# A large SBUF region moved from 64 bytes past a multiple of 128 to a multiple of 128, in a two-block transformer kernel

## What is computed

```python
# first block
h = rmsnorm(x) ; q, k, v, g, u, sv, a_ret, a_sgu = split(h @ w_in)
y_ret = (layernorm(retention(rotary(q), rotary(k), v)) * silu(g)) @ w_ret_o
y_sgu = (gelu(u) * (w_spatial mixed over layernorm(gelu(sv)) + b)) @ w_sgu_o
merged = sigmoid(a_ret) * y_ret + sigmoid(a_sgu) * y_sgu
x = x + rmsnorm(merged @ w_out)
a, b = split(conv3(rmsnorm(x) @ w_up) + conv_b)       # 1024 -> 2 * 2816
x = x + rmsnorm((gelu(a) * b) @ w_down)               # 2816 -> 1024
# second block: top-k sparse attention and sliding-window attention, gated
x = x + (sigmoid(g_a) * (o_a @ w_branch_a) + sigmoid(g_b) * (o_b @ w_branch_b)) @ w_out_2
x = x + relu(rmsnorm(x) @ w_up_2) ** 2 @ w_down_2     # 1024 -> 4096 -> 1024
return rmsnorm(x)
```

## Time and profile before

| | |
|---|---|
| time, median of 3 runs | 1735.6 us (1735.3 to 1737.29) |
| span of the profiled execution | 1735.5 us |
| instructions | 19726 |
| TensorE matmuls busy (PE) | 1653.0 us |
| TensorE weight loads busy (PEld) | 1347.8 us |
| VectorE (DVE) | 830.2 us |
| ScalarE (ACT) | 449.3 us |
| GpSimd (POOL) | 908.1 us |
| mean granted TensorE clock | 0.969 of full speed |

### The profile page before, as it was taken

How to read it: one execution, slowest core, us unless ns; L and a number is a source line. 1 busy time by engine, 2 the same in 40 slices (tenths; PEclk the granted TensorE clock), 3 DMA queues, 4 the chain that set the end, 5 groups by cost and what they waited for, 6 DMA issues and landing times.

```text
span 1735.5 us, 19726 instructions
## 1 busy us (share of the span) xinstructions
PE 1653.0 (95%) x7556; PEld 1347.8 (78%) x7556; DVE 830.2 (48%) x1094; ACT 449.3 (26%) x742; POOL 908.1 (52%) x336
## 2 busy tenths in 40 slices
PE   7999999999998999999989898589999899999998
PEld 6887888888887888888878776467677788888886
DVE  6702688510836666660032999944546532013302
ACT  3012112101114344441131222033331243123312
POOL 5873386877784444444474555403137544444442
PEclk9999999999999999999999999779899999999999
DMA  5332032332222333332212212101012222223221
GB/s 196 96 124 70 25 103 73 122 97 97 97 85 86 97 97 97 97 97 97 97 65 88 76 52 95 49 1 49 25 49 97 74 73 97 101 93 98 97 97 73
DMA packets 123281, 147.48 MB, mean 85 GB/s; under 512 B 5142, under 2 KB 98374, under 8 KB 123206
## 3 DMA queue, kind: packets, MB, share of 16 engines
q1 hardware_dynamic: 121622, 141.90, 25.3%
q10 hardware_dynamic: 1584, 4.52, 0.7%
HBM read 144.31 MB, written 2.10 MB: 84 GB/s over the span
## 4 chain that ended last, share of the span: by engine, by line
PE 82%; DVE 12%; POOL 3%; issue 2%; ACT 1%; DMA 0%; SPq 0%; DVEq 0%; POOLq 0%; ACTq 0%
PE ps L522 24%; PE ps L523 24%; PE ps L524 24%; PE ps L811 3%; PE ps L822 2%; DVE work L1516 2%; PE ps L701 2%; DVE top L1513 2%; DVE score L1505 2%; PE ps L816 1%; POOL w_lo L471 1%; PE ps L631 1%; POOL w_hi L462 1%; DVE m_lo L1401 1%; DVE rope_u L1273 1%
## 5 line engine op out<-in xcount | busy, mean ns | idle before, releaser
L471 POOL TENSOR_TENSOR w_lo<-raw,w_hi 128x1024 fp32r<-128x1024 f32 (+2 forms) x260 | 650.4, 2523 | 402.8 <-ACT w_hi L880 397.6
L462 POOL TENSOR_TENSOR w_hi<-raw,cells 128x2048 fp32r<-128x2048 f32 (+1 forms) x67 | 246.3, 3676 | 402.3 <-PE ps L522 402.3
L522 PE MATMUL ps<-hT_hi,w_hi 128*128 128x512 f32 (+1 forms) x960 | 372.3, 388 | 1.0 <-DVE hT_lo L1225 0.5
L523 PE MATMUL ps<-hT_lo,w_hi 128*128 128x512 f32 (+1 forms) x960 | 370.2, 386 | 0.0
L524 PE MATMUL ps<-hT_hi,w_lo 128*128 128x512 f32 (+1 forms) x960 | 369.6, 385 | 0.0
L522 PEld LDWEIGHTS ps<-hT_hi,w_hi 128*128 128x128 f32 x960 | 183.3, 191 | 38.4 <-issue 1.9
L524 PEld LDWEIGHTS ps<-hT_hi,w_lo 128*128 128x128 f32 x960 | 183.0, 191 | 35.6
L523 PEld LDWEIGHTS ps<-hT_lo,w_hi 128*128 128x128 f32 x960 | 183.3, 191 | 35.1
L880 ACT ACTIVATE w_hi<-raw 128x2048 fp32r<-128x2048 f32 x63 | 120.2, 1908 | 209.6 <-PE ps L522 207.9
L523 PE MATMUL ps<-w_lo,f_hi 128*128 128x512 f32 x432 | 170.2, 394 | 0.0
L522 PE MATMUL ps<-w_hi,f_hi 128*128 128x512 f32 x432 | 169.3, 392 | 0.0
(11 more groups left out here) (256 smaller groups left out, 2196.4 us busy)
## 6 DMA issues: line engine op xcount, KB each, us to landing
raw<-in_w_in SPq DMA_DIRECT2D x86, 512.0 KB, 4.5
raw<-in_w_up SPq DMA_DIRECT2D x76, 512.0 KB, 4.5
raw<-in_w_down SPq DMA_DIRECT2D x54, 512.0 KB, 4.0
raw<-in_w_out SPq DMA_DIRECT2D x16, 512.0 KB, 3.8
raw<-in_w_ret_o SPq DMA_DIRECT2D x8, 512.0 KB, 4.4
raw<-in_w_sgu_o SPq DMA_DIRECT2D x8, 512.0 KB, 4.4
x<-in_x SPq DMA_DIRECT2D x4, 512.0 KB, 7.4
raw<-in_w_branch_b SPq DMA_DIRECT2D x4, 512.0 KB, 4.4
```

Source lines behind the costliest of these rows:

```text
L462: nc.gpsimd.tensor_tensor(w_hi[:, s, 0:n], raw[:, s, 0:n], zero.broadcast_to([P, n]), ALU.add).then_inc(unit_hi, 1)
L471: nc.gpsimd.tensor_tensor(w_lo[:, s, c], raw[:, s, c], w_hi[:, s, c].bitcast(f32), ALU.subtract).then_inc(unit_split, 1)
L522: first = nc.tensor.matmul(dst, a_hi, b_hi, start=start, stop=False)
L523: nc.tensor.matmul(dst, a_hi, b_lo, start=False, stop=False)
```

## The change

`cells` gets 176 words instead of 192, so that the region behind it begins 64 bytes lower. The one cell in use beyond 176, `zero`, moves to an unused one.

```diff
         conv = at("conv", [P, 4, 2 * FB], small0 + 3072)
-        cells = at("cells", [P, 192], small0 + 3776)
-        A = small0 + 3776 + 768
+        cells = at("cells", [P, 176], small0 + 3776)
+        A = small0 + 3776 + 704
         eps = cells[:, 0:1]
...
-        zero = cells[:, 176:177]
+        zero = cells[:, 2:3]
```

## The result

| | before | after |
|---|---|---|
| median of 20 runs | 1736.62 us (1735.3 to 1737.98) | 1739.51 us (1737.72 to 1743.08) |
| span of the profiled execution | 1735.5 us | 1738.0 us |
| after / before, 95% interval | | 1.0016 [1.0011, 1.0022] |

The forecast was 1729.1 us, with a range of 1727.0 to 1736.0, and 0.05 for slower by over 0.2%. The result lies outside the range and on the other side: 1739.51 - 1736.62 = 2.9 us lost, with an interval of 0.11% to 0.22%. It is slower clear of noise, though by less than the 0.2% from which the prediction counts a version as slower. Instructions and their order on each engine are those of before.

What follows compares the result with a forecast made beforehand. TensorE was taken to bound the kernel, with the chain on it for 82% of the span. Gains of 1.26 + 1.26 + 0.96 + 1.06 + 0.34 + 0.85 + 0.79 = 6.5 us took 1735.6 to 1729.1 us, range 1727 to 1736.

Steps and rivals of the forecast that it cites:

- the distance between the operands is what counts: Rival: the penalty grows with the operands' distance inside 256 bytes and doubles, another 6.5 us lost, 1742.1 us; chance 0.05.
- the low bits don't matter: Rival: the address's low bits have no effect and nothing changes, 1735.6 us; chance 0.15. `iq_ik`'s pace was counted for it.
- terms 1 and 2: `y_ret` and `y_sgu`, streaming from `A`: each falls from 44.80 to 43.54 us, a gain of 1.26 us each.
- term 3: `out1`, holding `mT`: 146 matmuls before the chain leaves TensorE, by 6.6 ns, a gain of 0.96 us.
- Terms 4 to 6: Stages holding tiles from `A`: gains of 1.06 us in `down1`, 0.34 in `out2`, 0.85 and 0.79 in the two `down2`.
- `zero` at nothing: GpSimd's `w_hi`, which reads the moved cell `zero`: no cost taken, at most 4.8 us lost.
- VectorE and ScalarE at nothing: `oT_lo` on VectorE and `out_rows` on ScalarE, both in `A`: already as fast as in the fixed part, so no gain.
- Plain fp32 matmuls at nothing: TensorE's transposes, mix and attention values: no gain taken from alignment, though up to 0.9 us was possible.
- The doubt about `mT` and `f`: A penalty of the low bits alone should be equal for both held tiles, but is 6.7 and 2.2 ns.
- or at 240 (the distance does): Sign in `y_ret`: a pace of 240 ns means the distance counts, 233.3 ns that the low bits don't matter.

Runs made afterwards that it cites:

- Experiment 3: TensorE alone, none of the kernel's work: eight moving by eight stationary starts, 32 bytes apart within 256; 226.7 ns with both at 64, 232.7 with moving 128 and stationary 0.
- Experiment 9: TensorE alone, none of the kernel's work: fp32r matmuls with other column counts at several distances, and `iq_ik` at its own addresses; 328 columns spread over 6.6 ns, `iq_ik` took 151.0.
- experiment 1: TensorE alone, none of the kernel's work: stretches of 48 matmuls at the kernel's addresses before and after; holding `f` took 228.7 ns before, 233.3 after.
- change again: The changed kernel run and profiled once more, against the kernel before; 1739.73 us, ratio 1.0018 [1.0008, 1.0028].
- `A` at 448: Kernel before with `cells` packed into 112 words and `A` 256 bytes below the change's, again distance 128; 1739.77 us, ratio 1.0016 [1.0007, 1.0026].
- `zero` alone: Kernel before with only the cell `zero` moved, to cell 2; 1736.59 us against 1736.57, ratio 1.0001 [0.9992, 1.001].
- packed alone: Kernel before with `cells` packed into 112 words and `A` left at its place; 1736.77 us, ratio 1.0002 [0.9992, 1.0011].
- `A` at 640: Kernel before with `cells` packed into 112 words and `A` 64 bytes above `w` modulo 256 instead of 64 below; 1740.18 us, ratio 1.0023 [1.0014, 1.0033].
- `A` at 576: Kernel before with `cells` packed into 112 words and `A` 128 past a multiple of 256, like `w`: distance 0; 1729.46 us, ratio 0.9954 [0.994, 0.9967].
- The version with all at multiples of 256: Kernel before with `cells` packed into 112 words, `A` where the change put it and `BASE` raised by 128: distance 0; 1728.79 us, ratio 0.9955 [0.9941, 0.9968].
- the two controls: Kernel before with only `zero` moved (1736.59 us, ratio 1.0001), and with `cells` packed into 112 words but `A` in place (1736.77 us, ratio 1.0002).
- experiment 7: TensorE alone: chains of 96-matmul stages without pause at the addresses of before; `mT` took 233.4 ns after `yT`, 228.9 after `hT`.
- 6: TensorE alone: finer distances, fewer columns, plain fp32, and stages with all slots and PSUM banks; 512 columns of fp32r took 226.7 ns at distance 0, 232.3 at 4.

## Why the prediction was wrong

**The step that failed** is the one named as the step that it takes: that the move "gives each of the slow stretches the pace that the same shape has with both operands at multiples of 128, 226.7 ns". The earlier trace rows hold only three combinations, and in the fast one both operands lie 128 past a multiple of 256. "Both at a multiple of 128" and "both at the same place within 256 bytes" fit these rows equally well. The edit separates them: it puts `A` at a multiple of 256 and leaves `w` 128 from it. Experiment 3 decides for the second reading.

**The evidence against the right rival.** The prediction names it ("the distance between the operands is what counts"), gives it 0.05, and holds `iq_ik` against it: distances of 32 to 96 bytes at 150.5 ns. That 328 columns without a loss take about that long was the author's estimate; the rows of before hold no other pace at this column count to measure it by. Experiment 9 shows 150.0 at distance 0 for 328 columns, and more at 32 (153.3) but less at 224 (146.7), so the row could neither confirm nor exclude anything at 512. The same row was counted for "the low bits don't matter", as wrongly.

**The rival's price was off too.** It let the penalty grow with the distance, to 240 ns and 1742.1 us. The measured paces are 228.9 at 192 (233.3 for `mT`), 233.3 at 64 and 232.2 to 233.3 at 128. So what streams `oT` or `yT` went from one slow place to another and stayed (233.3), and only what holds `f` or `m` lost, 3.5 ns a matmul.

**The terms of the sum.** With the places right they were good. At distance 0 the gain is 1736.53 - 1729.46 = 7.1 us for 6.5 forecast, with an interval of 5.7 to 10.4, and the five stretches have the lengths that the terms assume. In the change, with minus for a gain: terms 1 and 2 (`y_ret`, `y_sgu`) came out at 0 for -1.26 each, term 3 (`out1`) at 0 for -0.96. Terms 4 to 6 changed sign: `down1` 482 matmuls by 3.5 ns, +1.69 for -1.06; `out2` 155 by 3.2 (from the 229.0 and 232.2 of its addresses in experiment 1), +0.50 for -0.34; the two `down2` 768 by 3.5, +2.69 for -1.64. By paces that makes 4.9 us, and 2.9 were measured.

**Where the other 2 us are.** The start or end of a stage in each profile, less the same in the profile of before, in us:

| | change, change again, `A` at 448 | `zero` alone, packed alone | `A` at 640 | `A` at 576 |
|---|---|---|---|---|
| end of `down1` | +1.59, +1.43, +1.58 | -0.26, -0.32 | +0.07 | -5.28 |
| first matmul of the second block (919.61 before) | +0.38, +0.19, +0.35 | -0.56, -0.58 | -0.08 | -5.19 |
| start of `y_a` (1293.96 before) | -0.17, -0.52, -0.41 | -0.72, -0.62 | +0.09 | -5.55 |
| start of the first `down2` | -0.13, -0.40, -0.33 | -0.52, -0.43 | +0.36 | -5.45 |
| end of the last `down2` | +2.56, +2.30, +2.37 | -0.52, -0.43 | +3.79 | -7.16 |

The loss of both `down2` (2 x 1.34 = 2.7) arrives in full. That of `down1` is there at its end and gone by the first `down2`, in all three profiles at distance 128. With `A` at 640 and at 576 what `down1` lost or gained is kept.

The boundary behind `down1` shows where 1.1 us of it come back. The rows run from the transposes (L631) of the last rows of `x` to the transposes that follow, in before, packed alone, the change and `A` at 640:

```profile
912.44:918.82 6.38, 6.38 (x21) 5.33 (x22) 2.68 (x4) 1.19 (x2) 0.00 (x0) 0.55 0.34 106
912.11:918.24 6.13, 6.13 (x21) 5.13 (x22) 2.69 (x4) 1.19 (x2) 0.00 (x0) 0.57 0.35 110
913.88:919.20 5.32, 5.32 (x21) 4.48 (x21) 2.69 (x4) 1.19 (x2) 0.00 (x0) 0.68 0.40 128
912.31:918.74 6.43, 6.43 (x21) 5.40 (x22) 2.69 (x4) 1.19 (x2) 0.00 (x0) 0.54 0.33 104
```

TensorE does the same work in each and has no gap. What differs is the granted clock: 0.55 of full speed before and 0.68 in the change. Before, TensorE had idled between the pieces of the boundary (busy for 0.62 us from 908.10 to 911.30), and its granted clock was 0.50 from 911.4 to 918.2 us, with 1.00 in the 0.4 us that follow. In the change it was 0.51 from 914.2 to 917.7 us, with 1.00 in the 0.4 us on either side. So the change starts this work 1.44 us late and ends it 0.38 us late. The change again and `A` at 448 take 5.29 us for it, `zero` alone 6.05, and `A` at 576 takes 6.38. The version with all at multiples of 256 takes 5.30, so the short stretch is not tied to distance 128. Why it is short in these four profiles is not shown, and no term of the prediction stands for it. The rest stays open: against the two controls the three lose another 0.4 to 0.7 us of their lag on the way to `y_a`, and the 0.50 us of `out2` don't show between `y_a` and the first `down2`.

**What else the prediction said.** `zero` at nothing (bound 4.8 us): right, 1.0001. VectorE and ScalarE at nothing: right, `oT_lo` has a median of 678 ns after for 681 before, and `out_rows` 1062 for 1062. Plain fp32 matmuls at nothing (bound 0.9): right, 429.2, 215.8 and 111.7 ns whatever the distance. The doubt about `mT` and `f` was a real one, and has its answer in experiment 7. The statement that the median of before lies 0.1 us above the profiled span compares two executions: wherever a run has both, its time is 1.8 us above its span (1739.82 and 1738.0 for the change). So the profile of before shows one of the slower executions, which fits the 0.4 to 0.5 us by which both controls lead it. The sign to look for, "or at 240 (the distance does)", would have been read wrongly: with `y_ret` at 233.3 the text says that low bits don't matter, while `f` at 232.4 shows that they do.

## What to carry to other kernels

When a matmul-bound kernel places its tiles by hand, work out for each kind of matmul the distance of the stationary from the moving operand modulo 256, and for fp32r with 512 columns make it 0; the alignment of each alone says nothing. If two rules fit the fast rows, look for what the edit makes that no row has, and measure that combination by itself first: here stretches of 48 matmuls on an otherwise idle core gave the sign, and all paces but `mT`'s within about 1 ns of the kernel's. The time of the whole kernel still came out 2 us from the sum of the paces. A row with another column count is no evidence for or against such a penalty.

## What the runs showed of the hardware

- Of fp32r matmuls with 512 columns, one after another, each with its own weight load, the pace is 226.7 ns at distance 0 and up to 234.3 at others, in a pattern that repeats every 256 bytes (within 1.1 ns; starts tried up to 221,312).
- Distances d and 256 - d differ: 64 takes 233.3 ns, 192 takes 228.9.
- Distance 192 has two paces that hold, 228.9 and 233.3, and what ran before chooses. It is not the only such place: at the same addresses distance 128 took 232.2 ns in experiments 3 and 6 and 233.3 in 9, and at 256 columns distance 64 took 113.3 in 6 and 117.8 in 9.
- The same work of TensorE at a boundary took 6.38 us at a granted clock of 0.55 and 5.32 at 0.68: started 1.44 us late in the change, it ended 0.38 us late.
- At 256 columns distance 0 is the slowest of the four that were tried (120.0 ns, for 113.3 to 118.7), at 320 columns all four took 146.7, and plain fp32 took 429.2 (512 columns), 215.8 (256) or 111.7 (128) at each of the distances 0, 64, 128 and 192.
